# One sum a half, last squares on VectorE and an earlier second half in the sublayer changes of a decoder trunk

## Chip, cores and metric

The kernel runs on one core of a Trainium2 chip. The metric is the device time of one execution in microseconds (us).

## What is computed

A decoder trunk of two layers for a prompt of 512 tokens and 8 samples of one token each, 520 columns in all, width 1024, in fp32. Layer 0 mixes tokens by a gated projection (SGU), layer 1 by latent attention (MLA) over a shared key/value side (KV); each is followed by a feed-forward network with a short convolution (ConvFFN). Each sublayer ends and begins with an RMS norm:

```python
def rms_norm(x, g):
    xf = x.astype(jnp.float32)
    y = xf * lax.rsqrt(jnp.mean(xf * xf, axis=-1, keepdims=True) + EPS)
    return (y * g.astype(jnp.float32)).astype(x.dtype)

for layer in range(DEPTH):
    if layer == N_A_LAYERS:
        ckv_new, kr_new = kv_side(x, ...)
    h = rms_norm(x, p['pre_mix_g'][layer])
    m = sgu_mixer(h, ...)            # layer 0
    m = mla_mixer(h, ...)            # layer 1
    x = x + rms_norm(m, p['post_mix_g'][layer])
    h = rms_norm(x, p['pre_ffn_g'][layer])
    f, cs = conv_ffn(h, ...)
    x = x + rms_norm(f, p['post_ffn_g'][layer])
```

## The kernel before

Activations lie transposed: features on the 128 partitions, the 520 columns along the free side, so a vector of width 1024 is KD = 8 tiles. The columns are worked on in two halves of HB = 260 (`HALF[0]`, `HALF[1]`), each with its own bank of an accumulator slot in `psum`. Every weight product is made of three matmuls in fp32r: high part of the weight times high part of the input, high times low, low times high (`product`, L714). The weights stream through a ring of four stages by SyncE; for each unit of at most eight 128x128 tiles ScalarE (ACT) writes the high part (L1348, L1351) and VectorE (DVE) the low part (L1848), two units ahead of TensorE (PE). `ahead_static(n)` is the split of unit n + 2. All queues are written out by hand, each engine works its own in order, and semaphores tie them.

A **sublayer change** (`update(p, ...)` on ACT and DVE, p = 1 after the SGU, 2 after the first ConvFFN, 3 after attention, 4 after the last ConvFFN) lies between the last product of one sublayer and the first of the next. Its parts:

- `last_units` on PE: the last output tile (for attention the last two) is computed half by half. Inside its second half, after two products, PE sums the squares of the whole sublayer output of the first half: `half_rms(name, 0)`, L773 and L775: a matmul of `ones` with `sqa` (the squares of the tiles so far, added up by DVE in `add_squares`), and one with `sq[:, 1]`, the last tile's square.
- ACT loads the table set of Ln and Exp (`roots`, L1365), squares the last tile from PSUM (`last_square`, L1397), makes r2 = exp(-0.5 ln(mean)) (`rms`, L1372 and L1374), copies the last tile scaled by its gain (`last_raw`, L1400), writes the high parts of the new x (`high`, L1430) and squares x for the next norm (`squares`, L1438).
- DVE multiplies the sublayer's output by r2 (`scaled`, L1886), adds it to x (`added`, L1892) and makes the low parts (`lows`, L1867). In attention it also adds the sixth tile's squares (`sixth_squares`, L2415), which are late too. It goes through one half and then the other. At the head of each half it waits for that half's r2.
- `triple_units` on PE: the first three units of the next sublayer start on the un-normalized x, tile by tile, in step with DVE: three units for the first half, two for the second, then the third unit's second half. Between them stand `half_rms(m_name, 1)`; the sums of x squared, which take 32 output columns a matmul so that four run beside each other (`sum_four`, L783, twice a half); and, after ACT has read those back (`gather_sums`, L1443), `sum_groups` (L790). r1 from these scales the products when DVE evacuates them (up projection L2090 to L2092; KV L2170).

After the KV change ACT and DVE also make the query input (`query_input`, L1647; `low_mix`, L1860); ACT does the first three tiles of it before the Ln and Exp of the second half of x2 (`ahead_of_norm`), the other five after.

In down projection each output tile takes four units (`DN_SPLIT`); for the last tile `DN_LAST` lists them as (first tile, number), the last two going through `last_units`. A unit's split on ACT waits for the unit before the last to be over, as its weights use the same slot.

Of the kernel before, what the change touches and what calls it, by code (L numbers as in the profile page):

```python
# [14 lines left out]
P = 128  # L15
# [39 lines left out]
DN_LAST = [(8, 4), (12, 4), (16, 6), (0, 8)]  # L55
# [18 lines left out]
SQA = {n: sum(c - 2 + (m == "m_attn" or m in ALL_ADDED) for m, c, _ in GROUPS_SQ[:i] if m not in ON_PE) for i, (n, _, _) in enumerate(GROUPS_SQ)}  # L74
# [110 lines left out]
def trunk(nc, a, outs):  # L185
    ctx = ExitStack()
    with ctx:
# [271 lines left out]

        def packed(eng, blocks, share=(0, 1)):  # L460
# [235 lines left out]
        def _(pe):  # L696
# [52 lines left out]
            def last_units(units, rh, rl, name):  # L749

                for h in range(2):
                    for i, (n, slot, ks, first, last, ready) in enumerate(units):
# [3 lines left out]
                        for kk, k in enumerate(ks):  # L756
                            mm = product(n, slot, weight_slot(n), k, kk, rh, rl, first and kk == 0, last and kk == len(ks) - 1, parts=(h,))
                            if h and (i, kk) == (0, 1):
                                half_rms(name, 0)
# [17 lines left out]
            def sum_four(name, h, g):  # L777

                if g == 0:
                    pe.wait_ge(ln_done, SSB[name] - 1 + h)  # L780
                pe.wait_ge(sq_done, SQB[name] + 4 * h + 2 * g + 2)
                for j in range(4):
                    mm = pe.matmul(psum[32 * j:32 * j + 32, 6 + h, 0:HB], ones[:, 0:32], pair_squares(2 * g + j // 2)[:, HALF[j % 2]],  # L783
                                   start=(g == 0), stop=(g == 1))
                mm.then_inc(sq_summed, 1)
# [6 lines left out]
            def triple_units(n, rh, rl, sem, base, m_name, x_name):  # L792
# [10 lines left out]
                for t in range(KD):  # L803
# [533 lines left out]
        def _(act):  # L1337
# [50 lines left out]
            def update(p, name, m, ahead_of_norm):  # L1388
# [22 lines left out]
                roots()  # L1411
# [164 lines left out]
            def wo(i):  # L1576
                for e in range(2):
                    t = 2 * i + e
                    ahead(U_WO, 4, i, 2 * e)
                    ahead(U_WO, 4, i, 2 * e + 1)  # L1580
# [16 lines left out]
            def mlp(l):  # L1597
# [24 lines left out]
                def down(i, e, guard=False):  # L1622
                    t = 2 * i + e
                    for w in range(4):
                        if guard:
                            ahead_static(U_DN[l] + 4 * t + w)
                        else:
# [23 lines left out]
            update(2, "m_ffn0", m_raw, lambda: query_input(0, 3))  # L1651
            query_input(3, KD)
# [168 lines left out]
            for t in range(KD):  # L1821
                ahead_static(U_O + t)
                if t < KD - 2:
                    act.wait_ge(mm_done, U_O + t + 1)
                    raw("m_attn", t, t % 2, m_attn[:, t, :], POST[3])
            ahead_static(U_UP[1])
# [16 lines left out]
        def _(dve):  # L1843
# [25 lines left out]

            def update(p, name, m, between=lambda: None):  # L1870
# [5 lines left out]
                for h in range(2):  # L1876
                    dve.wait_ge(r_ready, SSB[name] + h + 1)
# [20 lines left out]

                    if h == 0 and p < 4:
                        for t in range(2):  # L1900
# [7 lines left out]
                        scaled(4, 2)  # L1908
                        lows(2, 3)
# [3 lines left out]
                        added(6, 2)  # L1913
                        lows(6, 7)
# [540 lines left out]
```

## Time and profile before

| | us |
|---|---|
| three runs: lowest, median, highest | 1388.6, 1390.4, 1391.74 |
| the profiled execution | 1387.88 |
| its span, first to last instruction | 1386.1 |

| engine | busy us | share | instructions |
|---|---|---|---|
| PE (matmul) | 1368.9 | 99% | 11807 |
| PEld (weight load) | 1297.3 | 94% | 11807 |
| DVE | 892.5 | 64% | 1522 |
| ACT | 552.2 | 40% | 902 |
| POOL | 178.0 | 13% | 334 |

PE's granted clock is full over the whole span, in the page's 40 slices. Matmuls are pipelined, so a row's duration is longer than the step to the next row; what a matmul costs is the distance between starts. An fp32 matmul stands in the trace as two records, an fp32r one as one.

### The profile page before, as it was taken

The numbers are of one execution on the slowest core, as the hardware profiler recorded it, in microseconds if no ns is written. First come the engines' busy times: TensorE is split into PE (matmuls) and PEld (weight loads), VectorE is DVE, ScalarE is ACT, GpSimd is POOL, SyncE is SP. The second block draws the span as 40 slices with busy tenths as digits, with TensorE's granted clock in tenths as the row PEclk, the third lists the DMA queues.
The fourth block names the chain that finished last, engine by engine and source line by source line (L and its number), as shares of the span: only waits on it lengthen the run. The fifth ranks groups of instructions, "written<-read, shape, count | busy, mean of one in ns | idle before, by whom it ended". The sixth has DMA issues, their size and how long they took to land.

```text
span 1386.1 us, 30511 instructions
## 1 busy us (share of the span) xinstructions
PE 1368.9 (99%) x11807; PEld 1297.3 (94%) x11807; DVE 892.5 (64%) x1522; ACT 552.2 (40%) x902; POOL 178.0 (13%) x334
## 2 busy tenths in 40 slices
PE   8999999999999999999999999999999999999998
PEld 8999999999999999999999955559899999999998
DVE  5545665227888888833376697673688888883334
ACT  6545444236322222233376532563733222223334
POOL 2000000000223333210000220100022222221000
PEclk9999999999999999999999999999999999999999
DMA  7432222332233333232333675102323333323322
GB/s 225 130 92 85 71 73 74 93 92 77 83 100 91 91 91 91 65 100 85 92 107 107 258 270 189 51 1 62 91 77 91 91 91 91 91 68 101 86 87 78
DMA packets 224403, 138.17 MB, mean 100 GB/s; under 512 B 12670, under 2 KB 220702, under 8 KB 223288
## 3 DMA queue, kind: packets, MB, share of 16 engines
q1 hardware_dynamic: 219944, 113.34, 28.4%
q0 software_dynamic: 4112, 23.61, 4.5%
q8 instruction: 54, 0.88, 0.3%
q10 hardware_dynamic: 272, 0.15, 0.0%
q14 instruction: 21, 0.17, 0.0%
HBM read 133.78 MB, written 3.67 MB: 99 GB/s over the span
## 4 chain that ended last, share of the span: by engine, by line
PE 90%; DVE 4%; issue 1%; ACT 1%; DVEq 0%; ACTq 0%
PE psum L714 80%; DVE kt L2237 2%; PE psum L1129 1%; PE psum L1289 1%; PE psum L907 1%; PE psum L1264 1%; PE psum L1267 1%; PE psum L1090 1%; PE psum L1278 1%; PE psum L893 0%; PE psum L783 0%; PE psum L1112 0%; DVE small L2369 0%; PE psum L775 0%; PE psum L1327 0%
## 5 line engine op out<-in xcount | busy, mean ns | idle before, releaser
L1848 DVE TENSOR_TENSOR wl<-ws,wh 128x1024 fp32r<-128x1024 f32 x211 | 258.4, 1225 | 304.0 <-ACT wh L1351 174.5
L714 PE MATMUL psum<-xh,wh 128*128 128x260 f32 x1998 | 409.4, 284 | 1.0 <-DVE kvr L2170 0.4
L714 PE MATMUL psum<-xh,wl 128*128 128x260 f32 x1998 | 406.7, 283 | 0.0
L714 PE MATMUL psum<-xl,wh 128*128 128x260 f32 x1998 | 406.1, 283 | 0.0
L714 PEld LDWEIGHTS psum<-xh,wh 128*128 128x128 f32 x1998 | 310.0, 189 | 2.1 <-DVE ab L2092 0.7
L714 PEld LDWEIGHTS psum<-xh,wl 128*128 128x128 f32 x1998 | 310.0, 189 | 0.0
L714 PEld LDWEIGHTS psum<-xl,wh 128*128 128x128 f32 x1998 | 309.2, 189 | 0.0
L1351 ACT ACTIVATE wh<-ws 128x1024 fp32r<-128x1024 f32 x144 | 152.0, 1056 | 297.3 <-PE psum L714 297.2
L714 PE MATMUL psum<-acth,wh 128*128 128x260 f32 x704 | 147.6, 284 | 0.6 <-DVE wl L1848 0.6
L714 PE MATMUL psum<-acth,wl 128*128 128x260 f32 x704 | 146.2, 283 | 0.0
L714 PE MATMUL psum<-actl,wh 128*128 128x260 f32 x704 | 146.1, 283 | 0.0
L1348 ACT ACTIVATE wh<-ws 128x1024 fp32r<-128x1024 f32 x67 | 70.8, 1057 | 124.7 <-PE psum L714 124.7
L714 PEld LDWEIGHTS psum<-acth,wh 128*128 128x128 f32 x704 | 110.4, 189 | 1.3 <-DVE wl L1848 1.0
L714 PEld LDWEIGHTS psum<-actl,wh 128*128 128x128 f32 x704 | 110.6, 188 | 0.1
L714 PEld LDWEIGHTS psum<-acth,wl 128*128 128x128 f32 x704 | 110.4, 189 | 0.0
L1605 ACT ACTIVATE cc<-cc 128x536 f32<-128x536 f32 x44 | 28.7, 653 | 161.2 <-DVE cc L2111 161.2
L605 POOL COPY cs<-ab 128x2 f32 (+1 forms) x88 | 44.1, 501 | 345.1 <-DVE ab L2092 345.1
L2111 DVE SCALAR_TENSOR_TENSOR cc<-ab,pt,cc 128x536 f32<-128x536 f32 x88 | 68.4, 777 | 12.1 <-DVE cc L2108 4.7
L2108 DVE SCALAR_TENSOR_TENSOR cc<-ab,pt,cc 128x536 f32<-128x536 f32 x88 | 68.3, 776 | 12.2 <-DVE cc L2106 6.1
L2090 DVE TENSOR_TENSOR ab<-psum,r 128x260 f32<-128x260 f32 x88 | 37.6, 427 | 33.3 <-PE psum L714 22.3
L714 PE MATMUL psum<-ush,wh 128*128 128x260 f32 x256 | 54.6, 284 | 0.0
L606 POOL COPY cs<-ab 128x8 f32 (+1 forms) x88 | 54.3, 617 | 0.5 <-issue 0.3
(313 smaller groups left out, 1847.8 us busy)
## 6 DMA issues: line engine op xcount, KB each, us to landing
ws<-in_w_up SPq DMA_DIRECT2D x88, 512.0 KB, 3.8
ws<-in_w_in_a SPq DMA_DIRECT2D x32, 512.0 KB, 4.1
ws<-in_w_down SPq DMA_DIRECT2D x30, 384.0 KB, 3.3
ws<-in_w_down SPq DMA_DIRECT2D x28, 320.0 KB, 3.1
ws<-in_w_out_a SPq DMA_DIRECT2D x16, 512.0 KB, 3.8
ws<-in_w_o SPq DMA_DIRECT2D x8, 512.0 KB, 4.7
xn<-in_x_prompt SPq DMA_DIRECT2D x4, 512.0 KB, 7.8
ws<-in_w_dq SPq DMA_DIRECT2D x4, 512.0 KB, 6.2
```

Source lines behind the costliest of these rows:

```text
L605: pool.tensor_copy(cs[:, 0:2, bass.ds(f, 1)].rearrange("p k o -> p (k o)"), ab[:, u % 2, SEQ:SEQ + 2])
L606: pool.tensor_copy(cs[:, 2:2 + NS, bass.ds(f, 1)].rearrange("p k o -> p (k o)"), dst[:, :, 2]).then_inc(tails, 1)
L714: mm = pe.matmul(psum[:, 2 * slot + b, 0:HB], w, r[:, k, b * HB:(b + 1) * HB], start=st, stop=en)
L907: mm = pe.matmul(psum[:, 5, c * P:(c + 1) * P], vn[:, c, :], wmt[:, bass.ds(g, 1), :].rearrange("p o t -> p (o t)"), start=True, stop=True)
L1348: act.activation(weights(n)[0], ws[:, slot4, :], ACT.Copy).then_inc(w_high, 1)
L1351: act.activation(wh[:, slot2, :], ws[:, slot4, :], ACT.Copy).then_inc(w_high, 1)
L1605: act.activation(cc[:, 0, :], cc[:, 0, :], ACT.Gelu_apprx_tanh).then_inc(gelu_done, 1)
L1848: dve.tensor_tensor(low_, ws[:, slot4, :], f32(high), ALU.subtract).then_inc(w_low, 1)
L2090: dve.tensor_tensor(ab[:, b, 2:2 + HB], a_b[:, 0, 0:HB], r1[:, 0:HB], ALU.mult)
L2108: dve.scalar_tensor_tensor(out=cc[:, b, :], in0=ab[:, b, 1:1 + CW_], scalar=w[1], in1=cc[:, b, :], op0=ALU.mult, op1=ALU.add)\
L2111: dve.scalar_tensor_tensor(out=cc[:, b, :], in0=ab[:, b, 2:2 + CW_], scalar=w[2], in1=cc[:, b, :], op0=ALU.mult, op1=ALU.add)\
L2237: dve.transpose(kt[:, n % KRING, :, :].rearrange("p e (m b) -> p m e b", b=32), src.rearrange("p m (e a) -> p m e a", a=32)).then_inc(kt_r ...
```

## The change

It edits the four sublayer changes and the last down units.

- `DN_LAST`: the unit of 8 tiles comes before the one of 6.
- `half_rms`: DVE adds the last tile's square to `sqa` (`last_squares`, new), and PE makes one sum a half instead of two. Only the second half of the last change keeps two. The first half's sum stands after the fourth product of the second half, not the second. On DVE `last_squares(name, 0)` comes ahead of the last weight split of the sublayer (in attention together with `sixth_squares(0)`), `last_squares(name, 1)` in the first half between `scaled(4, 2)` and `lows(2, 3)`.
- `sum_eight` replaces two `sum_four`: all eight 32-column sums of a half after its last tile. `sum_groups` of the second half stands after tile 1 of the third unit instead of tile 2.
- `roots` goes one output tile ahead of the last (in attention after the fifth tile's copy).
- DVE: the second half's first product (`next_first`) is made ahead of `lows(6, 7)` of the first half, and the order inside the second half has one product fewer in front. ACT: `high(0, 3)` after one `squares`, not two, `high(1, 0)` ahead of the fourth, the gathering of sums ahead of `squares(4)`.
- KV: two tiles of query input ahead of the norm instead of three, and a low part between the two evacuations.

```diff
-DN_LAST = [(8, 4), (12, 4), (16, 6), (0, 8)]
+DN_LAST = [(8, 4), (12, 4), (0, 8), (16, 6)]
...
+        def last_added(name, h):
+
+            return SQA[name] + KD - 1 + h * (2 if name == "m_attn" else 1)
...
-                            if h and (i, kk) == (0, 1):
+                            if h and (i, kk) == (0, 3):
                                 half_rms(name, 0)
...
             def half_rms(name, h):
 
-                more = h if name == "m_attn" else 0
                 if h == 0:
-                    pe.wait_ge(sq_added, SQA[name] + KD - 2)
                     wait(pe, ln_done, SSB[name])
-                elif more:
-                    pe.wait_ge(sq_added, SQA[name] + KD - 1)
-                pe.matmul(psum[:, 6 + h, 0:HB], ones[:, :], sqa[:, HALF[h]], start=True, stop=False)
-                pe.wait_ge(sq_done, SQB[name] + KD + h + more)
-                pe.matmul(psum[:, 6 + h, 0:HB], ones[:, :], sq[:, 1, HALF[h]], start=False, stop=True).then_inc(ss_done, 1)
...
+                split_sum = name == "m_ffn1" and h == 1
+                if not split_sum:
+                    pe.wait_ge(sq_added, last_added(name, h))
+                mm = pe.matmul(psum[:, 6 + h, 0:HB], ones[:, :], sqa[:, HALF[h]], start=True, stop=not split_sum)
+                if split_sum:
+                    pe.wait_ge(sq_done, SQB[name] + KD + 1)
+                    mm = pe.matmul(psum[:, 6 + h, 0:HB], ones[:, :], sq[:, 1, HALF[h]], start=False, stop=True)
+                mm.then_inc(ss_done, 1)
+
+            def sum_eight(name, h):
+
+                pe.wait_ge(ln_done, SSB[name] - 1 + h)
+                pe.wait_ge(sq_done, SQB[name] + 4 * h + 4)
+                for g in range(2):
+                    for j in range(4):
+                        mm = pe.matmul(psum[32 * j:32 * j + 32, 6 + h, 0:HB], ones[:, 0:32], pair_squares(2 * g + j // 2)[:, HALF[j % 2]],
+                                       start=(g == 0), stop=(g == 1))
+                    mm.then_inc(sq_summed, 1)
...
-                    if t == 5:
-                        sum_four(x_name, 0, 0)
                 pe.wait_ge(m_ready, MB[m_name] + KD + (2 if m_name == "m_attn" else 1))
-                sum_four(x_name, 0, 1)
+                sum_eight(x_name, 0)
...
-                    if t == 6:
-                        sum_four(x_name, 1, 0)
-                sum_four(x_name, 1, 1)
+                sum_eight(x_name, 1)
                 for t in range(KD):
                     blocks(1, t, (2,))
-                    if t == 2:
+                    if t == 1:
                         sum_groups(x_name, 1)
...
                 squares(0)
+                high(0, 3)
                 squares(1)
-                high(0, 3)
                 squares(2)
+                high(1, 0)
                 squares(3)
-                high(1, 0)
+                high(1, 1)
                 ahead_static(LOCKED[p] + 1)
-                high(1, 1)
+                gather_sums(0)
                 squares(4)
-                gather_sums(0)
...
+            def last_squares(name, h):
+
+                more = h if name == "m_attn" else 0
+                dve.wait_ge(sq_done, SQB[name] + KD + h + more)
+                dve.wait_ge(sq_added, last_added(name, h) - 1)
+                dve.tensor_tensor(sqa[:, HALF[h]], sqa[:, HALF[h]], sq[:, 1, HALF[h]], ALU.add).then_inc(sq_added, 1)
+
...
+                    def next_first():
+
+                        dve.wait_ge(r_ready, SSB[name] + 2)
+                        dve.wait_ge(x_new, base + KD - 2)
+                        out, scale = (r[:, 0:n * HB].rearrange("p (e c) -> p e c", e=n) for r, n in ((ut[:, 0, :], 2), (r2[:, HALF[1]], 1)))
+                        dve.tensor_tensor(out, m[:, 0:2, HALF[1]], scale.to_broadcast([P, 2, HB]), ALU.mult).then_inc(u_mul, 2)
+
...
                         scaled(4, 2)
+                        last_squares(name, 1)
                         lows(2, 3)
                         added(4, 2)
                         scaled(6, 2)
                         lows(4, 5)
                         added(6, 2)
+                        next_first()
+                        lows(6, 7)
+                    elif p < 4:
+                        added(0, 2)
+                        scaled(2, 2)
+                        added(2, 2)
+                        scaled(4, 2)
+                        lows(0, 1)
+                        added(4, 2)
+                        scaled(6, 2)
+                        lows(2, 3)
+                        added(6, 2)
+                        lows(4, 5)
                         lows(6, 7)
...
-            update(2, "m_ffn0", m_raw, lambda: query_input(0, 3))
-            query_input(3, KD)
+            update(2, "m_ffn0", m_raw, lambda: query_input(0, 2))
+            query_input(2, KD)
...
+            sixth_squares(0)
+            last_squares("m_attn", 0)
             ahead_static(U_UP[1])
-            sixth_squares(0)
             update(3, "m_attn", m_attn, lambda: sixth_squares(1))
             mlp(1)
+            last_squares("m_ffn1", 0)
             update(4, "m_ffn1", m_raw)
```

## Rows read from the trace of the kernel before

**Rows 1.** The page, its part 4: share of the ending chain by engine.

```profile
PE 90%; DVE 4%; issue 1%; ACT 1%; DVEq 0%; ACTq 0%
```

**Rows 2.** Timeline of PE (start us, us, engine, line), SGU change, first-half sum.

```profile
316.30 0.28 PE L714 MATMUL psum<-ush,wl 128*128 128x260 f32 x1
...
317.60 0.29 PE L714 MATMUL psum<-usl,wh 128*128 128x260 f32 x1
```

**Rows 3.** The same timeline, second-half sum.

```profile
324.55 0.28 PE L714 MATMUL psum<-xh,w 128*128 128x260 f32 x1
...
325.67 0.29 PE L714 MATMUL psum<-xl,w_up 128*128 128x260 f32 x1
```

**Rows 4.** The same timeline, one sum of groups alone.

```profile
336.50 0.28 PE L714 MATMUL psum<-xh,w 128*128 128x260 f32 x1
336.61 0.60 PE L790 MATMUL psum<-sqa,ones 128*128 128x260 f32 x2
...
337.18 0.28 PE L714 MATMUL psum<-xl,w_up 128*128 128x260 f32 x1
```

**Rows 5.** The same timeline, products around four sums of 32 columns.

```profile
329.77 0.28 PE L714 MATMUL psum<-xh,w 128*128 128x260 f32 x1
...
330.78 0.28 PE L714 MATMUL psum<-xl,w_up 128*128 128x260 f32 x1
```

**Rows 6.** Timeline of PE, attention change, first-half sum; idle before and releaser in brackets.

```profile
978.20 0.28 PE L714 MATMUL psum<-xh,wl 128*128 128x260 f32 x1
979.30 0.70 PE L773 MATMUL psum<-sqa,ones 128*128 128x260 f32 x2 [0.83 <-DVE sqa L2415]
...
980.40 0.28 PE L714 MATMUL psum<-xl,wh 128*128 128x260 f32 x1
```

**Rows 7.** Timeline of PE, last down units of layer 0, first half.

```profile
701.10 0.28 PE L714 MATMUL psum<-acth,wl 128*128 128x260 f32 x1
...
701.90 0.28 PE L714 MATMUL psum<-actl,wh 128*128 128x260 f32 x1
```

**Rows 8.** Timeline of PE, end of the third unit, SGU change and KV change.

```profile
344.65 0.28 PE L714 MATMUL psum<-xh,w 128*128 128x260 f32 x1
...
345.42 0.40 PE L714 MATMUL psum<-xl,wh 128*128 128x260 f32 x2
...
732.83 0.28 PE L714 MATMUL psum<-xkh,w_kv 128*128 128x260 f32 x1
...
733.88 0.28 PE L714 MATMUL psum<-xl,wh 128*128 128x260 f32 x1
```

**Rows 9.** Timeline of ACT, SGU change.

```profile
310.20 1.06 ACT L1348 ACTIVATE wh<-ws 128x1024 fp32r<-128x1024 f32 x1 [4.70 <-PE psum L714]
...
315.20 1.28 ACT L1365 ACT_TABLE_LOAD   x1
316.49 0.39 ACT L1397 ACTIVATE sq<-psum 128x260 f32<-128x260 f32 x1
317.68 0.48 ACT L1372 ACTIVATE r<-psum,eps 128x260 f32<-128x260 f32 x1 [0.80 <-PE psum L775]
```

**Rows 10.** Timeline of DVE, SGU change (two rows) and attention change (two rows).

```profile
320.26 0.48 DVE L1867 SCALAR_TENSOR_TENSOR xl<-x,pt,xh 128x260 fp32r<-128x260 f32 x1
...
328.65 0.89 DVE L1867 SCALAR_TENSOR_TENSOR xl<-x,pt,xh 128x260 fp32r<-128x260 f32 x2 [1.18 <-ACT xh L1430]
...
976.36 2.36 DVE L1848 TENSOR_TENSOR w<-ws,w 128x1024 fp32r<-128x1024 f32 x2
978.82 0.43 DVE L2415 TENSOR_TENSOR sqa<-sqa,sq 128x260 f32<-128x260 f32 x1
```

**Rows 11.** PE's weighing of one sample, and the weight loads at L783 (min/median/max ns).

```profile
818.28 1.91 PE L1112 MATMUL psum<-lat,pts 128*32 128x256 f32 x32
...
L783 PEld LDWEIGHTS psum<-sqx,ones x48: 105/108/110, 330.0 to 1002.1; 128*32 128x32 f32 x48
```

**Rows 12.** Timeline of DVE, last change, its second half.

```profile
1375.77 1.31 DVE L1886 TENSOR_TENSOR ut<-m_raw,r 128x520 f32<-128x520 f32 x2 [0.52 <-ACT r L1374]
```

More of the change, by code:

```diff
@@ L73 @@
 ALL_ADDED = ("x0", "v", "kv", "cq")
-SQA = {n: sum(c - 2 + (m == "m_attn" or m in ALL_ADDED) for m, c, _ in GROUPS_SQ[:i] if m not in ON_PE) for i, (n, _, _) in enumerate(GROUPS_SQ)}
+SQA = {n: sum(c - 2 + (m == "m_attn" or m in ALL_ADDED) + 2 * (m in HALVED) for m, c, _ in GROUPS_SQ[:i] if m not in ON_PE) for i, (n, _, _) in enumerate(GROUPS_SQ)}
 SQB = {n: sum(c + (m in HALVED) + (m == "m_attn") for m, c, _ in GROUPS_SQ[:i]) for i, (n, _, _) in enumerate(GROUPS_SQ)}
@@ L765, in half_rms @@
             def half_rms(name, h):
-                more = h if name == "m_attn" else 0
                 if h == 0:
-                    pe.wait_ge(sq_added, SQA[name] + KD - 2)
                     wait(pe, ln_done, SSB[name])
-                elif more:
-                    pe.wait_ge(sq_added, SQA[name] + KD - 1)
-                pe.matmul(psum[:, 6 + h, 0:HB], ones[:, :], sqa[:, HALF[h]], start=True, stop=False)
-                pe.wait_ge(sq_done, SQB[name] + KD + h + more)
-                pe.matmul(psum[:, 6 + h, 0:HB], ones[:, :], sq[:, 1, HALF[h]], start=False, stop=True).then_inc(ss_done, 1)
[L777 to L785, printed above, removed]
+                split_sum = name == "m_ffn1" and h == 1
[14 more added lines that the diff above has]
+                    mm.then_inc(sq_summed, 1)
             def sum_groups(name, h):
@@ L1409, in sixth @@
                     act.activation(m[:, KD - 2, HALF[h]], psum[:, h, 0:HB], ACT.Copy, scale=pt[:, gain - 1:gain]).then_inc(m_ready, 1)
-                roots()
                 if p == 3:
@@ L1579, in wo @@
                     ahead(U_WO, 4, i, 2 * e)
+                    if isinstance(t, int) and t == KD - 2:
+                        roots()
                     ahead(U_WO, 4, i, 2 * e + 1)
@@ L1626, in down @@
                             ahead_static(U_DN[l] + 4 * t + w)
+                            if (t, w) == (KD - 2, 1):
+                                roots()
                         else:
@@ L1825, in _ @@
                     raw("m_attn", t, t % 2, m_attn[:, t, :], POST[3])
+                if t == KD - 4:
+                    roots()
             ahead_static(U_UP[1])
@@ L1876, in update, with ready @@
                 for h in range(2):
-                    dve.wait_ge(r_ready, SSB[name] + h + 1)
+                    def ready():
+                        dve.wait_ge(r_ready, SSB[name] + h + 1)
                     def scaled(t, n):
@@ L1897, in lows @@
                                 low_half(p, t, h)
+                    def next_first():
[3 more added lines that the diff above has]
+                        dve.tensor_tensor(out, m[:, 0:2, HALF[1]], scale.to_broadcast([P, 2, HB]), ALU.mult).then_inc(u_mul, 2)
                     if h == 0 and p < 4:
+                        ready()
                         for t in range(2):
@@ L1913, in update @@
                         added(6, 2)
+                        next_first()
[11 more added lines that the diff above has]
+                        lows(4, 5)
                         lows(6, 7)
                     else:
+                        ready()
                         scaled(0, 2)
@@ L1920, in update @@
                         scaled(4, 2)
-                        lows(0, 1)
                         scaled(6, 2)
                         added(4, 2)
-                        lows(2, 3)
                         added(6, 2)
-                        lows(4, 5)
-                        lows(6, 7)
                     dve.wait_ge(x_new, base + KD * (h + 1))
@@ L2058, in _ @@
             wo(3)
+            last_squares("m_sgu", 0)
             ahead_static(U_UP[0])
@@ L2160, in _ @@
             mlp(0)
+            last_squares("m_ffn0", 0)
             ahead_static(U_KV)
             update(2, "m_ffn0", m_raw)
-            for t in range(3):
+            for t in range(2):
                 low_mix(2, t)
@@ L2170, in _ @@
                 dve.tensor_tensor(halves(kvr[:, t, :]), acc(1 - t), halves(r1[:, :]), ALU.mult).then_inc(evac_kv, 1)
-            for t in range(3, KD):
+                low_mix(2, t + 2)
+            for t in range(KC + 2, KD):
                 low_mix(2, t)
```

## The prediction

> **What bounds the kernel now.** I read the page first, for the engine on which the chain that ended last lies; then the timeline of TensorE (PE) inside the four sublayer changes, for the distance from one matmul's start to the next; then ScalarE (ACT) and VectorE (DVE) there, for what PE waits on. PE is 90% of the chain [rows 1]. In the changes it runs on too, so PE time taken away there is time off the end, unless ACT or DVE then come late. The unit is the start-to-start step of the 128x260 product matmuls, 0.12 us (in rows 6 the last product before the gap and the two after the sums lie in that raster). Everything below is the excess of a stretch over n such steps.
>
> What the sums cost PE: two sums back to back take 324.55 to 325.67, less 2 steps: 0.88 us [rows 3]. One alone takes 336.50 to 337.18, less 2 steps: 0.44 us [rows 4]. So a full-width fp32 sum of a half costs 0.44 us and has no cost of its own for coming between products. A group of four 32-column sums takes 329.77 to 330.78, less 2 steps: 0.77 us [rows 5]. As its arithmetic is the same 260 columns, 0.44 us, 0.33 us of that is getting in and out of 32-column work.
>
> Where PE stands idle: at the first-half sum of the SGU change 316.30 to 317.60 is 1.30, less 0.24 and less the 0.88 of the two sums: 0.18 us of waiting [rows 2, 3]. At that of the attention change 978.20 to 980.40 is 2.20, less 1.12: 1.08 us, released by DVE's add at L2415 [rows 6]. Between the last two units of down projection 701.10 to 701.90 is 0.80, less 0.24: 0.56 us [rows 7]; the same stands before the last change, so twice. At the end of the third unit (n+2) 344.65 to 345.42 is 0.77, less 3 steps: 0.41 us, and in the KV change 732.83 to 733.88 is 1.05, less 0.36: 0.69 us; the change of layer 1 before up projection shows 0.41 again [rows 8]. There PE waits for the first evacuation, which waits for r1 of the second half.
>
> **Part by part.**
> (a) One sum a half instead of two. Of 8 places 7 lose one (the second half of m_ffn1 keeps two): 7 x 0.44 = 3.1 us off PE. In exchange DVE adds a 128x260 square, 0.43 us each [rows 10], 7 times. On the path it lies only if the sum waits for it. First half: the sum now stands after product 3 instead of 1, 6 steps or 0.72 us later. The square can start some 0.2 us after the half's last product, ends 0.39 later [rows 9], the add 0.46 after that: about 1.05 us after the second half has begun, and the sum is due at 1.44. No wait. Queued behind this add on DVE is one weight split (1.2 us), wanted only by the three units 4 us on. Second half: the add stands in DVE's queue between scaled(4,2) and lows(2,3), where DVE now has idle time until xh comes; PE asks for it after tile 1 of three units. For the SGU and attention changes it is there 0.3 to 0.6 us ahead. For the KV change it is about 0.1 late, see (f).
>
> (b) Root tables a tile sooner. The load takes 1.28 us on ACT just ahead of the last square, which starts only when it ends [rows 9]; that made the 0.18 us at SGU. One tile earlier ACT waits 4.70 us for PE [rows 9], so it is hidden; without that cover it would cost its 1.28 us on ACT and at most the 0.18 now seen. At the attention change the 1.08 us are mostly DVE: the pair of splits ends at 978.7 and only then comes the sixth tile's add, 978.82 to 979.25 [rows 10]. The diff puts both adds ahead of the split that belongs to U_UP[1]. With tables early the sixth square is done when the split before it ends, about 977.5, both adds by 978.5, and the sum is due at 979.0. So 0.18 + 1.08 = 1.3 us go.
>
> (c) DN_LAST swapped. The last unit's weights can be split only when the second but last but one (4 tiles) is over: high 1.06 + low 1.23 us and two hops is about 2.4 (a split on ACT and a pair on DVE: rows 9, 10). Today PE has 6 tiles x 3 x 0.12 = 2.16 us of first-half work meanwhile, with the swap 8 tiles, 2.88 us. The 0.56 [rows 7] goes twice: 1.1 us. That its waits add up to 0.46 plus 0.1 of getting going again says the weights come 2.6 us after the slot falls free: 0.25 of slack is left.
>
> (d) sum_four pairs become sum_eight, 6 times. If the second four follow the first without leaving 32-column work, a pair costs 0.77 + 0.44 to 0.49 (0.49 if each pass steps as the first two of a group do) instead of 1.54: 0.28 to 0.33 saved. The nearest row of many such groups one after another is the weighing of the samples, 32 records in 1.91 us: less the 0.38 of the last, 1.53 over 7 steps of four, 0.22 us each for 256 columns, loads hidden [rows 11]. I take 0.31: 1.9 us. The lower bound is that all overhead is paid again: 0.
> The Trainium skill, TensorE: Matmul & The Clock Gate, Part 3, says that a weight load overlaps running matmuls only when its row group differs; all of these share theirs. By it two more loads of 0.108 us each [rows 11] would show per pair and this part would be 0.6 instead of 1.9; the row of the weighing speaks against it.
>
> (e) The second half's sum_groups one tile earlier (t = 1 instead of 2) moves the chain to r1 0.36 us ahead relative to the third unit, and one tile less of query input stands before it in the KV change (0.65 us on ACT; with low_mix on DVE likewise). Today PE has the sum and 5 tiles x 3 products behind it, 0.44 + 1.80 = 2.24 us, then idles 0.31 (0.41 less 0.1 of getting going again): the chain takes 2.55. With the sum a tile sooner PE has 2.60: just covered. In the KV change the chain is 2.24 + 0.59 = 2.83 today and 0.2 to 0.3 shorter with the third query input gone. I count all three waits, 0.41 + 0.69 + 0.41 = 1.5 us, and keep 0.2 of them in the range. The gather for that sum ends some 0.25 us before PE wants it, so no new wait there.
>
> (f) Second half begun early, lower parts later. The product of tiles 8, 9 (m times r2) moves ahead of lows(6,7). At lows(6,7) DVE stands idle 1.18 us today waiting for ACT's xh [rows 10]; the diff also takes one pair of squares from before high(0,3), so xh comes 0.5 us sooner, and the 0.61 us fit. But the second half's additions then start 0.7 us earlier against the squares of x, of which sum_eight wants all four, with high(1,0) ahead of the fourth. I laid ACT's and DVE's queues out in their new order with the durations of rows 9 and 10, 0.04 us a hop, from the start of the second half. (The old order laid out so meets the trace to 0.1 us at each change.) From the sum's start it is 0.60 us to its result [rows 4], 3.06 us from Ln's start to the end of the first xl [rows 9, 10], in all 3.7; PE has 0.44 + 12 tiles x 0.36 = 4.8 us of other work before it at SGU and attention, but 0.44 + 3.6 = 4.0 at KV. So it holds, narrowly at KV. Further on the layout shows new waits at KV for the second square's add (0.14), for the fourth square (0.12) and for xl of the third tile (0.13), at attention 0.2 for the latter, each with 0.1 to get going again: 0.9 us, against 0.5 us of the same kind for that tile today, which go. Net 0.4 us lost.
>
> (g) Tail. At the last change 0.44 (one sum) + 0.56 come off PE. But the first half's chain on DVE starts only 0.44 + 0.56 - 0.72 = 0.28 earlier, since its sum stands 0.72 later in the order. Today DVE ends its first half 0.5 us before the second starts; so it now ends it at about 1374.97, and the second half, today from 1375.77 [rows 12], starts at about 1375.0. r2 is no longer what is late, DVE's own first half is. 0.77 of the 1.0 arrives: 0.24 lost. From there the output chain is unchanged.
>
> **Sum**: 3.1 + 1.3 + 1.1 + 1.9 + 1.5 = 8.9; less 0.4 (f), less 0.24 (g): 8.2 us. The profiled execution took 1387.88 us (span 1386.1), so 1379.7 for such a one; the median of the three runs is 1390.4, 2.5 above it, and I carry the difference over: 1390.4 - 8.2 = **1382.2 us**. Outside the four changes nothing is edited, and PE is without waits there, so the rest only shifts.
>
> **Rivals.**
> 1. Weight loads of the second four show (the rule in (d)): 6 x 2 x 0.108 = 1.3 us less, gain 6.9, 1383.5 us. The weighing row is against it. Chance 0.10.
> 2. DVE becomes the bound of the changes. It gets 7 x 0.43 us more in queues whose slack I have at 0.1 to 0.5 us, and PE is 1.5 to 2.5 us sooner in each. If every hop is 0.1 us longer than laid out, over some ten hops, each of three changes loses 1 us more: gain 5.2, 1385.2 us. For it: the margins at KV. Against: the old order is met to 0.1. Chance 0.16.
> 3. The change does little: waits merely move, since r1 and the xl tiles are set by DVE and ACT chains of unchanged length; only the sums' 3.1 minus (f), (g) remains, 2.5 us, 1387.9 us. Against: PE, not the chains, holds all but a few tenths of each change. Chance 0.05.
> 4. Slower: the early product waits for r2 of the second half at the head of DVE's queue, with lows(6,7) behind it, and PE needs these for tile 6. By the layout r2 is ready 0.1 us after DVE is free for it and PE's slack at tile 6 is 0.1 (KV) to 0.7 us. It decides from there: if Ln and Exp of that half came over 0.7 us later, each 1 us is 1 us of PE in each of three changes. To lose all 8.2 and 2.8 more takes 3.7 us + slack per change; with r2 late by 4.5 us it would be about 1394. Nothing queued before Ln on ACT is of that size. Chance 0.03.
> The forecast has 0.66.
>
> **Range and chances.** A measurement of this kernel tells about 0.2%, 2.8 us, from no change (the three runs lie 3.1 us apart). The forecast's own bounds: (d) 1.7 to 2.0, (e) -0.2, (f) 0.2 to 1.0, and 1 us for the runs: 1380.5 to 1384. Taking in rivals 1 and 2 with their run spread: 1380.2 to 1386.8; outside it rivals 3 and 4 and the tails. Faster by over 0.2% (under 1387.6): forecast, 1, 2 and a part of 3: 0.91. Same 0.06, slower 0.03.
>
> **What would show it.** Right: two records instead of four at the half sums and PE steps of 0.68 there; no idle at L773 in attention; 16 records at L783 with under 1.3 us excess; 0.12 us steps at the last down units and at the first product after the third unit; PE between the second half of the last unit and that product shorter by about 2.2, 1.8 and 2.8 us (SGU, KV, attention). Wrong: PE idle released by xl, xkl or sqa, DVE without gaps from L1886 to L1867 in the second half, or an excess of 1.5 at L783.

## The result and the profile after

The changed kernel took 1380.44 us (median of four runs, 1380.09 to 1380.64) against 1389.5 us before (1387.25 to 1391.74), a ratio of 0.9942 (95% interval 0.9931 to 0.9954). The forecast was 1382.2, with a range of 1380.2 to 1386.8. Run again later beside the kernel before it took 1380.43 against 1388.66: 8.2 us, the forecast gain; the 9.1 us of the first set are in part its high median of before. The time itself lies 1.8 us under the forecast and 0.24 us inside the range. The profiled execution took 1380.38 us; lines of its page (span, busy time, part 4: share of the ending chain):

```profile
span 1378.3 us, 30494 instructions
...
PE 1362.9 (99%) x11793; PEld 1294.3 (94%) x11793; DVE 894.8 (65%) x1529; ACT 553.0 (40%) x902; POOL 177.8 (13%) x334
...
PE 89%; DVE 5%; ACT 1%; issue 1%; DVEq 0%; ACTq 0%
```

14 PE records are gone (seven sums of two records each) and 7 DVE instructions have come; PE still holds the chain, with one point of it gone to DVE [rows 1].

**Where the time went.** I cut both traces where PE takes the first product on a new input. Stretches with an edit stand in bold.

| stretch of PE | before | after | gain |
|---|---|---|---|
| start to first SGU product | 15.68 | 15.81 | -0.13 |
| to first product of the SGU's output projection | 209.94 | 209.58 | +0.36 |
| **to first product on x1 (first-half sum)** | 96.88 | 96.24 | **+0.64** |
| **x1 to first down product (rest of the SGU change, up)** | 259.10 | 257.55 | **+1.55** |
| **to first KV product (swap, first-half sum)** | 129.07 | 127.98 | **+1.09** |
| **KV products to query input (rest of the KV change)** | 22.87 | 21.86 | **+1.01** |
| query input to cq | 24.01 | 24.43 | -0.41 |
| cq to the attention's output projection | 179.61 | 180.01 | -0.41 |
| **to first down product of layer 1 (attention change)** | 307.23 | 304.49 | **+2.74** |
| **to ACT's last copy of an output** | 138.27 | 137.58 | **+0.69** |
| last copy to the end of the span | 3.42 | 2.74 | +0.68 |

The bold stretches gain 7.7 us and the one behind the KV change gives 0.41 back: 7.3 us by the edit. The last line is the sending of the outputs, which lay anywhere from 2.7 to 3.4 us in the profiles of all kernels here, whatever their edit. With it and the three other unedited stretches the sum is the span's 7.8.

**Single sums and eight sums.** Timeline of PE after the change (start us, us, engine, line, operation), SGU change:

```profile
316.77 0.28 PE L718 MATMUL psum<-ush,wl 128*128 128x260 f32 x1
316.89 0.60 PE L776 MATMUL psum<-sqa,ones 128*128 128x260 f32 x2
317.14 0.47 PE L718 MATMUL psum<-ush,wh 128*128 128x260 f32 x1
317.45 0.28 PE L718 MATMUL psum<-usl,wh 128*128 128x260 f32 x1
...
330.62 0.28 PE L718 MATMUL psum<-xh,w 128*128 128x260 f32 x1
330.83 0.65 PE L788 MATMUL psum<-sqx,ones 128*32 128x260 f32 x8
331.29 0.62 PE L788 MATMUL psum<-sq,ones 128*32 128x260 f32 x8
331.84 0.39 PE L718 MATMUL psum<-xh,w_up 128*128 128x260 f32 x1
332.06 0.28 PE L718 MATMUL psum<-xl,w_up 128*128 128x260 f32 x1
...
342.57 0.28 PE L718 MATMUL psum<-xh,w 128*128 128x260 f32 x1
342.69 0.46 PE L718 MATMUL psum<-xh,wh 128*128 128x260 f32 x2
342.99 0.40 PE L718 MATMUL psum<-xl,wh 128*128 128x260 f32 x2
```

The half sum stands as one pair of records: 316.77 to 317.45 is 0.68, less two steps 0.44, as a sum alone took in [rows 4], and the wait of [rows 2] is gone. The eight sums follow each other as two groups 0.46 us apart; from 330.62 to 332.06 less two steps they cost 1.20 us, where two groups apart cost 2 x 0.77 [rows 5]. Behind the third unit the next product follows after 0.12 us; of the 0.41 of [rows 8] nothing is left.

Attention change, first-half sum and third tile of the second half, the same view (in brackets the idle time before and its releaser):

```profile
975.22 0.28 PE L718 MATMUL psum<-xh,wl 128*128 128x260 f32 x1
975.34 0.60 PE L776 MATMUL psum<-sqa,ones 128*128 128x260 f32 x2
975.59 0.47 PE L718 MATMUL psum<-xh,wh 128*128 128x260 f32 x1
975.90 0.28 PE L718 MATMUL psum<-xl,wh 128*128 128x260 f32 x1
...
991.65 0.28 PE L718 MATMUL psum<-xh,w 128*128 128x260 f32 x1
992.09 0.39 PE L718 MATMUL psum<-xh,w_up 128*128 128x260 f32 x1 [0.16 <-DVE xl L1873]
992.31 0.28 PE L718 MATMUL psum<-xl,w_up 128*128 128x260 f32 x1
```

The 1.08 us of [rows 6] are gone; a wait for the low part of the third tile has come, 991.65 to 992.31 less two steps: 0.42 us.

### The profile page after: what moved, and what is told of

It is laid out like the page before. It is cut to its first block, busy times and chain, and to the rows that moved or that the text cites. A ratio compares the mean times of both kernels' runs of the same rounds, so it can differ in the third digit from the quotient of the medians.

```text
span 1378.3 us, 30494 instructions
## 1 busy us (share of the span) xinstructions
PE 1362.9 (99%) x11793; PEld 1294.3 (94%) x11793; DVE 894.8 (65%) x1529; ACT 553.0 (40%) x902; POOL 177.8 (13%) x334
## 4 chain that ended last, share of the span: by engine, by line
PE 89%; DVE 5%; ACT 1%; issue 1%; DVEq 0%; ACTq 0%
PE psum L718 80%; DVE kt L2273 2%; PE psum L1130 1%; PE psum L1290 1%; PE psum L908 1%; PE psum L1265 1%; PE psum L1268 1%; DVE ut L1900 1%; PE psum L1279 1%; PE psum L894 0%; DVE x L1906 0%; PE psum L1091 0%; PE psum L1113 0%; PE psum L1328 0%; PE psum L788 0%
```

## Experiments

Each variant starts from the changed kernel, if nothing else is said. Runs vary by a microsecond or more, more than most effects here, so each is read from its profile by the stretches of the table above, against the changed kernel's. The code cuts are shortened. That this works is shown by the changed kernel run again:

**e9, the changed kernel again.**

> The changed kernel once more, as the companion of e10 on the same chip: 8 us under the kernel before. Its change segments should repeat to 0.05 us; the stretch before the output projection of the SGU and the attention phase (query products to the output projection's first) have moved by up to 1.4 and 0.6 us from profile to profile whatever the edit, and should do so again.

Measured: 1380.43 us (1379.31 to 1382.17, five runs), 0.9944 of before (0.993 to 0.9957). Every edited stretch repeats to 0.05 us, while the unedited one from cq to the output projection came out 0.63 us shorter. What is under 0.05 us in an edited stretch is no effect.

**e1, two sums a half again** (DVE's four `last_squares` gone, the order otherwise kept):

```diff
-pe.matmul(psum[:, 6 + h, 0:HB], ones, sqa[:, HALF[h]], start=True, stop=True)
+pe.matmul(psum[:, 6 + h, 0:HB], ones, sqa[:, HALF[h]], start=True, stop=False)
+pe.matmul(psum[:, 6 + h, 0:HB], ones, sq[:, 1, HALF[h]], start=False, stop=True)
```

> The changed kernel with the half sums back at two matmuls each (the add of the last square on VectorE taken out, places kept). Theory A, every sum taken off TensorE is worth its 0.44 us: 7 x 0.44 = 3.1 us longer. Theory B, VectorE's queue sets part of the time of the KV and attention changes: the sum costs TensorE 0.44 but VectorE is rid of 0.34 and waits of 0.1 to 0.4 shrink. Laid out: SGU +0.9, KV +0.2, attention +0.6, last change +0.4, in all +2.1 us; the idle time at the second-half sum of the KV change (0.31) and that at the third tile of the second half (0.4 in KV and attention) shrink or go.

Measured: 1383.73 us in one run. The stretches lose 0.44 and 0.33 (SGU, first and second half), 0.45 (KV, first half, before the first KV product), -0.31 (the rest of the KV change), 0.45 (attention) and 0.44 (last): 1.8 us, and not the 3.1 of seven sums. PE's rows at SGU show both sums back whole, 0.43 each. At KV the second-half sum costs only 0.13 more than in the changed kernel, and the waits for the fourth square and for the third tile (0.11 and 0.32) are gone: 0.14 in all for two sums. At attention the wait for the third tile goes too, and one sum of two is left. The edit gives PE its sums back and takes the adds of 0.43 us off DVE at once, so it prices the exchange as a whole and not PE's part of it.

**e2, four and four sums** (the first four after tile 7 of 8, the others after the last):

```diff
+                    if t == 6:
+                        sum_eight(x_name, 0, 0)
...
-                sum_eight(x_name, 0)
+                sum_eight(x_name, 0, 1)
```

> The changed kernel with the eight 32-column sums of a half split into four and four again, with one tile's products between. Theory A: each of the six splits costs the 0.33 us of leaving and entering 32-column work again, 2.0 us. Theory B (KV and attention wait for VectorE anyway and swallow part of the first half's split): SGU +0.6, KV +0.3, attention +0.3, in all +1.2 us. Rival, the second four pay their weight loads beside the first four too: then the split costs under 0.15 each, 0.9 at most, which the excess of 1.21 us at the eight already speaks against.

Measured: 1382.32 us in one run; SGU 0.58, KV 0.30, attention 0.33, together 1.2 us, where six times 0.33 would be 2.0. At SGU all of it arrives (two pairs), at the other two only one pair of two: the wait for the third tile takes in the other.

**e12, the eight sums alone, in the kernel before** (`sum_four` pairs to `sum_eight`, nothing else).

> The kernel before with sum_eight for the two sum_four alone. Theory A, TensorE's time is the sum: 6 x 0.33 = -2.0 us. Theory B, with VectorE's second half begun late as in the kernel before, what the first half's merge saves comes back as a longer wait for the lower part of the third tile of the second half (0.16 to about 0.5 us): only the second half's merge counts, 3 x 0.32 = -1.0 us. Then the early second half (e6) is what makes the first half's merges worth anything.

Measured: 1387.42 us in one run; 0.34, 0.35 and 0.30 us gained at the three changes, 1.0 in all, half of the 2.0 that PE is relieved of. The third tile of the second half shows where the rest stays. Timeline of PE in this variant:

```profile
334.98 0.28 PE L714 MATMUL psum<-xh,w 128*128 128x260 f32 x1
335.49 0.39 PE L714 MATMUL psum<-xh,w_up 128*128 128x260 f32 x1 [0.23 <-DVE xl L1863]
335.72 0.28 PE L714 MATMUL psum<-xl,w_up 128*128 128x260 f32 x1
```

334.98 to 335.72 is 0.74 us for two steps; before it was 0.40 there. In the changed kernel, whose second half begins earlier, both pairs arrive at SGU (e2), here one of two. At KV and attention e2 too has one of two.

**e3, the old order of the last down units.**

```diff
-DN_LAST = [(8, 4), (12, 4), (0, 8), (16, 6)]
+DN_LAST = [(8, 4), (12, 4), (16, 6), (0, 8)]
```

> The changed kernel with DN_LAST in its old order. Theory: the last unit's weights come 2.6 us after its slot falls free, TensorE has 2.16 instead of 2.88 us of work, so 0.57 us of waiting comes back in each layer, +1.1 us, and nothing else moves. Rival, the wait was for the weights' transfer: then the order makes no difference. Rival, the later waits of the KV change swallow it: +0.6.

Measured: 1381.99 us in one run; 0.55 before the KV change and 0.57 before the last, 1.1 us as summed in (c).

**e11, the swap alone, in the kernel before.**

> The kernel before with the exchange in DN_LAST alone. Theory: 0.57 us less in each layer, -1.1 us, at the last down units alone; all later waits stay as they were.

Measured: 1388.0 us in one run; 0.08 us in layer 0 and 0.54 in the last. In layer 0 the wait only moves. Timeline of ACT in this variant, then of PE:

```profile
704.14 1.06 ACT L1348 ACTIVATE w_kv<-ws 128x1024 fp32r<-128x1024 f32 x1 [0.67 <-DMA ws<-in_w_dkv]
705.22 1.28 ACT L1365 ACT_TABLE_LOAD   x1
706.51 0.39 ACT L1397 ACTIVATE sq<-psum 128x260 f32<-128x260 f32 x1
```

```profile
706.04 0.60 PE L773 MATMUL psum<-sqa,ones 128*128 128x260 f32 x2
706.96 0.71 PE L775 MATMUL psum<-sq,ones 128*128 128x260 f32 x2 [0.32 <-ACT sq L1397]
```

PE comes 0.56 us sooner, but ACT is held by a DMA for w_dkv and then by the table load, so the last square comes at 706.51 as late as ever and the second sum waits for it. In the changed kernel, with the tables a tile sooner, the same swap is worth 0.55 (e3): in layer 0 (c) needs (b), and as e4 shows, (c) makes (b) worth more.

**e4, the tables late again** (`roots` at the head of the last unit's copies, as before).

```diff
+                roots()
                 if p == 3:
...
-                if t == KD - 4:
-                    roots()
```

> The changed kernel with the tables loaded at the start of each change again. Theory: with one sum a half the last square's way now passes through VectorE, so the late load costs more than before: SGU +0.3 us (it was 0.18 in the kernel before), KV +0.1 to +0.5 depending on the split that waits for its transfer, attention +0.9, last change 0 (ScalarE idle there); in all +1.3 to +1.7. Rival: the load hides in the 0.72 us by which the sum was moved back, at most +0.2 in all, and the attention gain came from VectorE's order alone.

Measured: 1382.55 us in one run; 0.43 at SGU, 0.84 before KV, 1.07 at attention: 2.35 us, more than the 1.3 that (b) took out of the kernel before. At attention it is the same 1.08. At SGU it is 0.43 and not 0.18: the sum now needs the last square and then an add of 0.43 on DVE, and is due only 0.72 later. The 0.84 stands where (b) had named no gain; before the swap PE came there 0.56 later.

**e7, the two adds behind the last weight split at attention.**

```diff
+            ahead_static(U_UP[1])
             sixth_squares(0)
             last_squares("m_attn", 0)
-            ahead_static(U_UP[1])
```

> The changed kernel with the two adds on VectorE before the attention change behind the weight split of U_UP[1] again, as in the kernel before. Theory: the first-half sum waits 0.5 to 0.6 us for them; +0.5 to +0.7 us, at that place alone. Together with e4 this splits the 1.08 us of waiting seen there before. Rival: with the tables early the adds are in time behind the split as well: 0.

Measured: 1381.19 us in one run; 0.78 us, all at the attention change. So of its 1.08 the place in DVE's queue and the early table are both needed.

**e6, the early product late** (`next_first` behind `lows(6, 7)`).

```diff
-                        next_first()
                         lows(6, 7)
+                        next_first()
```

> The changed kernel with the early product of the second half behind the last two lower parts instead of ahead of them. Theory B: VectorE has it in the way of the second half's first additions, the fourth square is late and TensorE waits for it: SGU +0.7 , KV +0.7, attention +0.7, in all +2.1 us. Theory A, the place makes no difference as TensorE is the bound: 0 to +0.3. Rival 4 of the prediction (the early product costs more than it gives): shorter than the changed kernel.

Measured: 1383.77 us in one run; 0.83 at each of the three changes, 2.5 us. PE in this variant waits ahead of the eight sums:

```profile
331.29 0.28 PE L718 MATMUL psum<-xh,w 128*128 128x260 f32 x1
331.95 0.65 PE L788 MATMUL psum<-sqx,ones 128*32 128x260 f32 x8 [0.38 <-ACT sq L1438]
```

and ACT makes that square late because it waits for x of the second half:

```profile
330.36 0.92 ACT L1430 ACTIVATE xh<-x,pt 128x260 fp32r<-128x260 f32 x2 [0.95 <-DVE x L1906]
331.18 0.62 ACT L1438 ACTIVATE sq<-x 128x520 f32<-128x520 f32 x1
```

The chain is DVE's product and addition, ACT's high part and square, then PE. Without the early product, asking for all four squares at once costs this wait.

**e5, a price for DVE time at that place** (the early product made twice, 0.73 us more on DVE a change).

```diff
+                        dve.tensor_tensor(out, m[:, 0:2, HALF[1]], scale..., ALU.mult).then_inc(xT_done, 1)
+                        dve.wait_ge(xT_done, 9 + p)
                         dve.tensor_tensor(out, m[:, 0:2, HALF[1]], scale..., ALU.mult).then_inc(u_mul, 2)
```

> The changed kernel with the early product of the second half made twice on VectorE, one after the other, in each of three changes: 0.73 us more in VectorE's queue ahead of the last two lower parts. This prices the margin of that queue. Theory B, VectorE binds KV and attention and is near it at SGU: laid out +0.55, +0.6 and +0.6, in all +1.7 us, as waits for the fourth square (eight sums) and for tile 6 of the first half. Theory A, the 1.2 us of idle time seen there in the kernel before still cover it: 0 to +0.3 in all.

Measured: 1382.11 us in one run; 0.65, 0.82 and 0.69, 2.2 us for 3 x 0.73. DVE's queue from the early product on is now on the path in all three changes, with less than 0.1 us of slack at SGU and attention and none at KV. At KV the longest new wait, 0.54 us, is for the low part of the first half's seventh tile, which stands behind the early product.

**e8, the new waits mended** (in DVE's second half `lows(2, 3)` ahead of `scaled(6, 2)`, ACT's fourth square ahead of `high(1, 0)`, behind the KV change the add of squares ahead of the third evacuation).

```diff
-                        scaled(6, 2)
                         lows(2, 3)
+                        scaled(6, 2)
...
-                high(1, 0)
                 squares(3)
+                high(1, 0)
...
-            dve.tensor_tensor(halves(krr[:, :]), acc(2), halves(r1[:, :]), ALU.mult).then_inc(evac_kv, 1)
             add_squares(dve, "kv", 1, 1)
+            dve.tensor_tensor(halves(krr[:, :]), acc(2), halves(r1[:, :]), ALU.mult).then_inc(evac_kv, 1)
```

> The changed kernel with three exchanges in the order of instructions: in the second half on VectorE lows(2, 3) ahead of scaled(6, 2); on ScalarE the fourth square ahead of high(1, 0); after the KV change the squares' sum of kv on VectorE ahead of the evacuation of krr. Theory B (these queues are late, not TensorE): the waits for the third tile (0.4 us in KV and in attention) and for the fourth square (0.1 in KV) go, laid out 0.7 us, up to 0.9; and the 0.43 us that TensorE waits for the kv sum go too: 1.1 to 1.3 us shorter than the changed kernel. Theory A: nothing, since what is saved at one wait comes back at the next.

Measured: 1380.5 us (1379.63 to 1381.59, five runs), 0.9943 of before (0.9929 to 0.9956). The stretches gain 0.10, 0.29 and 0.28. The waits for the third tile and the fourth square, 0.53 us at KV and 0.42 at attention, are gone, but 0.24 and 0.16 of this come back two tiles on: at the sum of groups PE now loses 0.68 us at KV and 0.60 at attention where it lost 0.44, and the load of the fifth tile's weights (722.25 at KV) is released by DVE's low part, L1873. So DVE, which has the same work in another order, is late there instead. The third edit gave nothing. I had taken the gap at the KV sums for a wait of the sums for `sqa`. PE in the changed kernel:

```profile
734.60 0.40 PE L718 MATMUL psum<-xh,wl 128*128 128x260 f32 x2
734.84 1.14 PE L832 MATMUL psum<-sqa,ones 128*128 128x260 f32 x4
736.07 0.47 PE L718 MATMUL psum<-xh,wh 128*128 128x260 f32 x2
```

In e8 the sums run through, and the gap stands behind them, with a name:

```profile
735.56 1.04 PE L832 MATMUL psum<-sqa,ones 128*128 128x260 f32 x4
736.79 0.48 PE L718 MATMUL psum<-xh,wh 128*128 128x260 f32 x2 [0.19 <-DVE wl L1854]
```

The wait is for the weight split of the second query unit. DVE in the changed kernel works the split behind the evacuation and the add:

```profile
733.49 0.69 DVE L2210 TENSOR_TENSOR krr<-psum,r 128x520 f32<-128x520 f32 x1
734.10 0.68 DVE L456 TENSOR_TENSOR sqa<-sq 128x520 f32<-128x520 f32 x1
734.71 1.21 DVE L1854 TENSOR_TENSOR wl<-ws,wh 128x1024 fp32r<-128x1024 f32 x1
```

It ends at 735.92; PE starts on those weights at 736.07. The same place in the kernel before, DVE and then PE:

```profile
737.35 0.69 DVE L2174 TENSOR_TENSOR krr<-psum,r 128x520 f32<-128x520 f32 x1
737.96 0.69 DVE L456 TENSOR_TENSOR sqa<-sq 128x520 f32<-128x520 f32 x1
738.57 1.22 DVE L1848 TENSOR_TENSOR wl<-ws,wh 128x1024 fp32r<-128x1024 f32 x1
```

```profile
739.40 1.04 PE L831 MATMUL psum<-sqa,ones 128*128 128x260 f32 x4
740.09 0.59 PE L714 MATMUL psum<-xh,wh 128*128 128x260 f32 x2
```

There the split ended at 739.79, 0.3 us before PE wanted it. PE has come 4.56 us forward there and DVE only 3.86, so 0.3 us of slack became 0.43 of waiting.

**e10, mended with the split forward** (as e8, but the order is add, split, evacuation).

```diff
             add_squares(dve, "kv", 1, 1)
             ahead_static(U_KV + 2)
+            dve.tensor_tensor(halves(krr[:, :]), acc(2), halves(r1[:, :]), ALU.mult).then_inc(evac_kv, 1)
             ahead_static(U_DQ)
```

> As e8, but after the KV change VectorE's order is: squares' sum of kv, weight split of the second query unit, then the evacuation of krr. In e8 the 0.43 us did not go but moved behind the sums: TensorE waits for that split, which stood behind both. Theory: the wait was always the split's; with 0.61 us less in front of it, it goes (0 to 0.1 left), on top of the 0.7 us of e8: 1.1 us under e9. Rival: the evacuation of krr now late makes a wait of its own at the second or third query unit: 0.7 us under e9.

Measured: 1379.63 us (1378.94 to 1379.84, five runs), 0.9934 of before (0.9921 to 0.9948). Behind the KV change 0.47 us come back. Timeline of PE, then of DVE:

```profile
734.83 1.04 PE L832 MATMUL psum<-sqa,ones 128*128 128x260 f32 x4
735.52 0.59 PE L718 MATMUL psum<-xh,wh 128*128 128x260 f32 x2
```

```profile
733.48 0.70 DVE L456 TENSOR_TENSOR sqa<-sq 128x520 f32<-128x520 f32 x1
734.09 1.22 DVE L1854 TENSOR_TENSOR wl<-ws,wh 128x1024 fp32r<-128x1024 f32 x1
735.23 0.70 DVE L2212 TENSOR_TENSOR krr<-psum,r 128x520 f32<-128x520 f32 x1
```

With 0.09, 0.01, 0.30 and 0.26 in the changes this is 1.1 us by the stretches; the medians of the same chip lie 0.8 us apart (1380.43 and 1379.63), with intervals that overlap. It is the fastest of the kernels run; that it beats the changed one is shown by the profiles' stretches, not by the run times alone.

## Why the prediction was right, and where its steps were not

The three changes from the last unit's second half to the product behind the third unit were to be shorter by 2.2, 1.8 and 2.8 us; they are by 2.19 (0.64 + 1.55), 1.53 (1.09 + 1.01 less 0.57 of the swap) and 2.74. The 1.8 does not follow from the prediction's own terms, which give 1.66 at KV: 0.88 (a), 0.62 (d), 0.69 (e), less 0.69 of new waits, and 0.16 of an old one.

| step | forecast | measured in the two traces |
|---|---|---|
| (a) seven sums | 3.1 | 7 x 0.44 = 3.07 off PE |
| (b) waits at the first-half sums | 1.3 | 0.18 + 1.08, and 0.09 before KV: 1.35 |
| (c) last down units | 1.1 | 2 x 0.57 = 1.14 |
| (d) eight sums | 1.9 | 6 x 0.33 = 2.0 |
| (e) waits behind the third unit | 1.5 | 1.5, but 0.07 left at KV |
| (f) waits of the early second half, net | -0.4 | -0.76 |
| (g) tail | -0.24 | -0.31 |
| second query unit | 0 | -0.43 |
| sum | 8.2 | 7.6; by the stretches 7.3 |

**(a)** The size per sum held to 0.01, and the added squares hold up the sum at one place, second half of KV: its excess is 0.745 against 0.44, a wait of 0.31 where (f) had 0.14 plus 0.1. But e1 shows that the seven sums, exchanged for adds on DVE, are worth 1.8 us as a part of the changed kernel, not 3.1: at KV and attention PE waits for DVE afterwards. The prediction priced (a) and these waits (f) as separate terms. **(b)** and **(c)** held in size, but I priced them as independent. e4 and e11 show that they are not: the early tables are worth 2.35 in the changed kernel, and the swap without them 0.6 instead of 1.1. The prediction had one order of adding them up in which this does not show.

**(d)** held, and it was the disputed one. The second four start 0.46 us after the first and the pair costs 1.20 to 1.21: 0.33 saved, the upper end of 0.28 to 0.33. Rival 1 is refuted at its place: from the forecast's 1.54 - 0.31 = 1.23 a pair, loads that show would have made 1.23 + 2 x 0.108 = 1.45. In these fp32 sums of 32 columns side by side the weight loads, which take 0.11 us each [rows 11], lie behind the matmuls though all share a row group. The Trainium skill, TensorE: Matmul & The Clock Gate, Part 3, says that a load overlaps only when its row group differs; these rows speak against it. The same Part of the Trainium skill also lets a load into the background weight buffer run ahead, and no row here tells the buffer of a load. The Trainium skill, TensorEngine Tiling (Array Packing), Key Properties, says that switching modes requires a drain. The 0.33 us of entering and leaving, paid once now instead of twice, would fit that; no row names their cause.

**(e)** held in all three places, to 0.07 us at KV. **(f)** was the mis-sized term. Its list of waits was right, place by place; their sizes were 0.31, 0.11 and 0.42 at KV and 0.42 at attention, 1.26 us, where I had 0.9; the 0.5 of the old waits did go (0.05 is left at SGU). The layout gave 0.13 and 0.2 for the third tile, plus 0.1 each, and it is 0.42 twice; the fourth square it had 0.1 too long. So the layout, with 0.04 us a hop, came out 0.1 to 0.2 us short for the low parts. That it met the old order to 0.1 may be since PE, not this chain, was late there; no run tests that. **(g)** Of 1.0 us 0.69 arrived; DVE's second half now starts at once behind its first, as said. Timeline of DVE, last change:

```profile
1367.26 1.30 DVE L1906 TENSOR_TENSOR x<-x,ut 128x520 f32<-128x520 f32 x2
1368.65 1.31 DVE L1900 TENSOR_TENSOR ut<-m_raw,r 128x520 f32<-128x520 f32 x2
```

The 0.52 us of idle time in [rows 12] is gone.

**The step that failed** (beside the size of (f)) is the sentence "Outside the four changes nothing is edited, and PE is without waits there, so the rest only shifts". The rest shifts only if all engines come forward alike, or have slack for the difference. PE came 0.7 us further forward than DVE at the end of the KV change, and a weight split that had been 0.3 us early was late, 0.43 us; e8 showed which instruction it was and e10 took it away. The last row but one of the table is what this cost.

**Rivals.** Rival 2, DVE as the bound, is true in its mechanism and wrong in its price: e5 shows that 0.73 us more on DVE costs 0.65 to 0.82, so the slack is gone, but what had come by then was 0.8 us in the changes and 0.43 behind KV, and not 3. Two of the signs named for a wrong forecast did appear: waits of PE for xl, xkl and `sqa`, and at all three changes DVE goes through its second half without a gap that has a releaser. Rival 3, waits that merely move, is refuted as the whole account by the waits of (b), (c) and (e) being gone; in part it is true, since by e1 1.3 of the 3.1 us of (a), and by e2 0.8 of the 2.0 of (d), would otherwise be waits. Rival 4 decides from the early product being late: e6, which has it late, loses 2.5 us and stays 4.8 us faster than the kernel before (1383.77 against 1388.61), so it was never near.

**The forecast's 8.2 us** agree with the medians of all runs (1388.66 and 1380.43). The forecast time does not: I carried over the 2.5 us between the median of before and its profiled execution, while in the changed kernel these lie 0.06 apart and the later medians of before are 1388.6. That is most of the 1.8 us by which the forecast time was too high, and the measured time was nearly out of the range. By the traces, the edit explains 7.3 of them; the other 0.9 are within what single runs and unedited stretches vary by, and so the closeness of the total is in part luck. Of the 0.3 us between the sum of the terms and the stretches, 0.07 are what is left of (e); the rest has no place that I could name.

## What to carry to other kernels

When parts of a change all shorten one engine's work, price them together at each next wait: where a helper is late, what one part frees comes back as that engine's longer wait. Here the eight sums and the swap were worth half when made alone, the seven single sums 1.8 of 3.1 us when taken back last, and the early tables 1.7 times what they had freed. Check the stretch behind an edited one too: an engine that comes forward by more than its helpers eats slack that the old trace shows only as "no wait". And a wait whose releaser the profile does not name can be found by moving one candidate ahead of the other and seeing where the gap reappears.

## What had not been expected of the hardware

- Eight fp32 sums of 32 output columns next to each other cost 1.20 us for 260 columns each, two groups of four apart 2 x 0.77; inside, the two groups start 0.46 us apart, about what one full-width fp32 matmul takes (0.44).
- A table load took 1.28 us and the square behind it started at once (705.22 and 706.51 in e11). The Trainium skill, ScalarE: Activation LUTs, What ACT_TABLE_LOAD costs, counts about 2.66 us with a drain; no drain is seen between these rows.
- Stretches without an edit differ between profiles of like kernels: 225.2 to 226.8 us up to the SGU's output projection, 179.4 to 180.6 from cq to the attention's, 2.7 to 3.4 for sending the outputs. Edited stretches repeat to 0.05 us. Effects of some tenths can be had from stretches and not from the totals.
